# Memory updates, value copies, output gate and sample heads of a recurrent decoder's mixers, moved between engines and steps

## The chip, the core and the metric

The kernel runs on one core of a Trainium2 chip. Five engines work side by side, each through its own list of instructions in order: TensorE (PE, matrix products), VectorE (DVE), ScalarE (ACT), GpSimd (POOL) and SyncE (SP, which issues most transfers). They wait for each other on semaphores that the program sets by hand. The metric is the device time of one launch in microseconds (us); the median of three runs counts.

## What is computed

A two-layer decoder trunk for 256 prompt tokens and 8 sample sequences of 8 tokens, 320 columns in all, with the same weights. Each layer is a SwiGLU feed-forward part, a norm, one input projection, two mixers side by side (an RWKV-7 time mixer with 8 heads of 64 and an mLSTM with 4 heads of 128), an output projection, a norm, a second feed-forward part and a norm. All in fp32. The part of the reference that the change touches is the mLSTM's end of a chunk:

```python
num = g_inter[..., None] * einsum('bhtd,bhde->bhte', qc, C) + einsum('bhts,bhse->bhte', s, vc)
h = num / maximum(abs(den), exp(-m_t))[..., None]
C = dec[..., None, None] * C + einsum('bhs,bhsd,bhse->bhde', ws, kc, vc)
...
h = ((h - mu) * rsqrt(var + MH_EPS)).reshape(B, T, D_B) * mh_g
out = sigmoid(o_pre) * h
```

For the samples, `C` is a memory of 128 x 128 for each of 8 sequences and 4 heads, read from memory and written back with the layer's update. The RWKV-7 mixer is brought to a chunk form: per chunk of 64 tokens a triangular inverse is grown in six doubling levels, and a recurrence over four prompt chunks follows.

## The kernel before, in words

Each weight is split into a high and a low part (`whi` by ScalarE, `wlo` by VectorE) and multiplied in three passes (lines 2087 to 2089); the feed-forward parts and projections are such products. Between the input and the output projection of each layer lie the mixers, and there all that the change touches.

**The order of the mixers** is written out by hand. `tensor_mixers` (L916), `scalar_mixers` (L1226), `vector_mixers` (L1662) and `pool_mixers` (L1871) each run the same 27 steps, n = 0 to 26, one for each pair of level and chunk of the triangular inverse (five chunks, the fifth for the samples, with three levels). In a step n from 5 on TensorE makes a product (L735), VectorE masks it (L1684, `t1`), TensorE makes a growth from it in the next step (L747, L750), and ScalarE copies the growth (L1159); a growth waits for the copy of the one before. Steps 0 to 4 have a first growth only (L721, L724). All other work of the mixers hangs into these steps by tuples such as `WEIGHTS_AT`: the engine does it in that place of its list.

- **Side work** through bank 7 (`side` L666, `copy_side` L1127): TensorE turns or multiplies something, one of the other engines copies it out, and the next may start only then (`side_copied`). Number 0 is the tail of the projection, 1 to 5 the value tiles of the five chunks (copied into `uv`, two copies of 64 x 256, L1136), 6 to 10 the keys, 11 to 13 products of scores and values (`RVS`), 14 the last rows of the convolution (`ENDS`), 15 to 18 the states of the samples (`MEMS`).
- **The mLSTM** works in three tiles: two of 128 prompt tokens and one of the 64 sample tokens. Per tile TensorE makes scores (`tile_scores`, steps 9 and 14, the first ahead of step 0), VectorE the logarithms of weights (`tile_logs`), ScalarE exponentials (`tile_weights` L1086, in steps 4, 10, 15 at the end of the step), VectorE their product with the scores (`tile_products` L1447, steps 6, 11, 16), TensorE the numerators (`tile_values`, steps 7 and 12, `samples_of_heads`, steps 17 and 18). The tiles' heads are then normalised: means by VectorE (L1494), squares by ScalarE (L1109), spreads by VectorE (L1514), root by ScalarE (L1118), scaling by VectorE (L1528); group 0 is the prompt's 8 heads of 128 rows, group 1 the samples' 4 heads of 64 rows.
- **Left-overs** (`LEFT` L627, `left_over` L631, `left_over_done` L1538): thirteen small jobs through banks 4 to 6 in turn. "C" is the update of half a head's sample memories (a product of 64 x 128 by 64 x 512, then an addition by VectorE to `C0`), "H" turns a tile's heads back and VectorE multiplies them with the output gate `og`, "N" and "T" make and turn the normalisers. A job waits until the one three before has been taken from its bank.
- **The output gate** (`output_gate` L1078): a sigmoid over 128 x 1280 and four scalings with gains, by ScalarE ahead of step 0. Sigmoid, exponential and square root each need another table set, which the ScalarE loads.
- **POOL** makes the masks of values (L1848), multiplies the sample memories by their decays (L1855, eight operations, each awaited by the update of its half head through `memory_decayed`) and four memory terms of the RWKV-7 states (L1863, two operations each). It waits for semaphores in between, and it also issues output transfers.

The **recurrence** (`recurrence` L840, `scalar_recurrence`, `vector_recurrence`) follows the steps: for each of four chunks a product with the state, one with the inverse, one for the new state (L879), with copies by VectorE and ScalarE between. The left-overs 11 and 12 lie in its first chunk. SP sends a head's memories out when its second half is done (L2067), and waits for all of them before it loads the output projection's weights into the same place.

## Time and profile before

| | us |
|---|---|
| median of 3 runs (1552.19 to 1558.36) | 1557.95 |
| the profiled execution's own time | 1557.53 |
| its span, first to last instruction | 1555.8 |
| TensorE busy, of the span | 1487.7 (96%) |
| VectorE busy | 982.4 (63%) |
| ScalarE busy | 699.0 (45%) |
| POOL busy | 392.6 (25%) |
| mixers of layer 0, from the last product of the input projection to the end of the recurrence | some 379 to 507 |
| mixers of layer 1 | some 1144 to 1269 |

The difference between own time and span lies around the first and the last instruction. A busy TensorE is not TensorE at its peak: matrix products are pipelined, and the clock that they are granted is one of two levels, 2.4 GHz (1.00 in the profile) or 1.2 GHz (0.50). The rows that the prediction reads stand in a section of their own below.

### The profile page before, as it was taken

The numbers are of one execution on the slowest core, as the hardware profiler recorded it, in microseconds if no ns is written. First come the engines' busy times: TensorE is split into PE (matmuls) and PEld (weight loads), VectorE is DVE, ScalarE is ACT, GpSimd is POOL, SyncE is SP. The second block draws the span as 40 slices with busy tenths as digits, with TensorE's granted clock in tenths as the row PEclk, the third lists the DMA queues.
The fourth block names the chain that finished last, engine by engine and source line by source line (L and its number), as shares of the span: only waits on it lengthen the run. The fifth ranks groups of instructions, "written<-read, shape, count | busy, mean of one in ns | idle before, by whom it ended". The sixth has DMA issues, their size and how long they took to land.

```text
span 1555.8 us, 34010 instructions
## 1 busy us (share of the span) xinstructions
PE 1487.7 (96%) x13394; PEld 1430.9 (92%) x13394; DVE 982.4 (63%) x1519; ACT 699.0 (45%) x1200; POOL 392.6 (25%) x423
## 2 busy tenths in 40 slices
PE   8999999999888999999999999989998799999995
PEld 7999998999767999999999999979988589999995
DVE  4444445587265877775577775466854667877644
ACT  4333335755544543334443334366574355333332
POOL 4222472011441422220512221300143404222100
PEclk9999999999986999999999999999999799999998
DMA  8554543453113745454545545534421334545451
GB/s 216 148 149 148 164 148 81 133 139 83 31 32 91 193 136 148 143 153 150 155 126 148 155 139 165 153 96 119 120 58 30 108 92 143 174 137 159 150 163 34
DMA packets 318938, 198.82 MB, mean 128 GB/s; under 512 B 7792, under 2 KB 303760, under 8 KB 318832
## 3 DMA queue, kind: packets, MB, share of 16 engines
q1 hardware_dynamic: 315120, 190.69, 42.2%
q0 software_dynamic: 3712, 6.62, 2.1%
q8 instruction: 78, 1.28, 0.4%
q14 instruction: 28, 0.23, 0.0%
HBM read 188.50 MB, written 8.78 MB: 127 GB/s over the span
## 4 chain that ended last, share of the span: by engine, by line
PE 85%; DVE 7%; ACT 4%; DVEq 2%; issue 1%; DMA 0%; SPq 0%; ACTq 0%
PE bank L2087 23%; PE bank L2089 23%; PE bank L2088 23%; DVE wlo L2578 2%; PE bank L2174 1%; DVE rlo L2609 1%; ACT whi L2377 1%; PE bank L735 1%; PE bank L458 1%; PE bank L2179 1%; ACT z L1159 1%; PE bank L643 1%; PE bank L2138 1%; PE bank L747 1%; PE bank L750 1%
## 5 line engine op out<-in xcount | busy, mean ns | idle before, releaser
L2377 ACT ACTIVATE whi<-raw 128x1024 fp32r<-128x1024 f32 x340 | 358.2, 1059 | 470.5 <-PE bank L2089 451.4
L2578 DVE TENSOR_TENSOR wlo<-raw,whi 128x1024 fp32r<-128x1024 f32 x340 | 421.6, 1244 | 228.5 <-ACT whi L2377 227.7
L2087 PE MATMUL bank<-rhi,whi 128*128 128x322 f32 x984 | 306.5, 311 | 0.0
L2089 PE MATMUL bank<-rhi,wlo 128*128 128x322 f32 x984 | 305.9, 311 | 0.0
L2088 PE MATMUL bank<-rlo,whi 128*128 128x322 f32 x984 | 304.8, 310 | 0.0
L2087 PE MATMUL bank<-xh,whi 128*128 128x320 f32 x912 | 285.5, 313 | 4.1 <-DVE xl L2752 3.0
L2088 PE MATMUL bank<-xl,whi 128*128 128x320 f32 x912 | 282.4, 310 | 0.0
L2089 PE MATMUL bank<-xh,wlo 128*128 128x320 f32 x912 | 282.4, 310 | 0.0
L2847 POOL TENSOR_TENSOR hl<-scratch,hh 128x320 f32 x88 | 146.6, 1666 | 495.3 <-DVE scratch L2699 379.8
L2087 PE MATMUL bank<-hh,whi 128*128 128x320 f32 (+1 forms) x704 | 218.4, 310 | 0.5 <-DVE wlo L2578 0.5
L2089 PE MATMUL bank<-hh,wlo 128*128 128x320 f32 (+1 forms) x704 | 217.4, 309 | 0.0
L2088 PE MATMUL bank<-hl,whi 128*128 128x320 f32 (+1 forms) x704 | 217.4, 309 | 0.0
L2088 PEld LDWEIGHTS bank<-rlo,whi 128*128 128x128 f32 x984 | 186.5, 189 | 0.0
L2087 PEld LDWEIGHTS bank<-rhi,whi 128*128 128x128 f32 x984 | 185.5, 189 | 0.0
L2089 PEld LDWEIGHTS bank<-rhi,wlo 128*128 128x128 f32 x984 | 185.5, 189 | 0.0
L2087 PEld LDWEIGHTS bank<-xh,whi 128*128 128x128 f32 x912 | 172.3, 189 | 9.3 <-issue 6.3
L2088 PEld LDWEIGHTS bank<-xl,whi 128*128 128x128 f32 x912 | 172.4, 189 | 0.5
L2089 PEld LDWEIGHTS bank<-xh,wlo 128*128 128x128 f32 x912 | 172.3, 189 | 0.0
L2087 PEld LDWEIGHTS bank<-hh,whi 128*128 128x128 f32 x704 | 132.4, 188 | 1.3 <-issue 1.0
L2088 PEld LDWEIGHTS bank<-hl,whi 128*128 128x128 f32 x704 | 132.4, 188 | 0.2
L2089 PEld LDWEIGHTS bank<-hh,wlo 128*128 128x128 f32 x704 | 132.4, 188 | 0.0
L2680 DVE TENSOR_TENSOR scratch<-bank,scratch 128x322 f32<-128x322 f32 x132 | 65.0, 493 | 71.5 <-PE bank L2089 63.8
(420 smaller groups left out, 1963.9 us busy)
## 6 DMA issues: line engine op xcount, KB each, us to landing
raw<-in_ffn_wg SPq DMA_DIRECT2D x88, 512.0 KB, 3.8
raw<-in_ffn_wu SPq DMA_DIRECT2D x88, 512.0 KB, 3.8
raw<-in_ffn_wd SPq DMA_DIRECT2D x88, 512.0 KB, 3.6
raw<-in_w_in SPq DMA_DIRECT2D x60, 512.0 KB, 3.8
raw<-in_w_out SPq DMA_DIRECT2D x16, 512.0 KB, 5.5
raw<-in_state_C SPq DMA_DIRECT2D x8, 512.0 KB, 6.1
out_s_C<-raw SPq DMA_DIRECT2D x8, 512.0 KB, 3.9
ring<-in_state_wkv POOLq DMA_DIRECT2D x8, 256.0 KB, 5.1
```

The source lines that it names most:

```text
L458: return pe.matmul(out, src, ident[0:rows, 0:rows], start=True, stop=True)
L643: last = pe.matmul(b[:, :], kt[PART[q], 2, 2 * g, :], vmask[g][PART[q], 4 * half:4 * half + 4, :], start=True, stop=True)
L735: last = pe.matmul(bank[n % 2][PART[1 - q], j * CH:(j + 1) * CH], ati[part, c, j, :], xi(q, c, j), start=True, stop=True)
L747: pe.matmul(bank[2 + q][PART[q], j * CH:(j + 1) * CH], xti(q, c, j), t1[PART[1 - q], c, j, :], start=True, stop=True)
L750: last = pe.matmul(bank[2 + q][PART[1 - q], j * CH:(j + 1) * CH], t1[PART[1 - q], c, j, :], xti(q, c, j), start=True, stop=True)
L2087: pe.matmul(out, w_hi, hi, start=start, stop=False)
L2088: pe.matmul(out, w_hi, lo, start=False, stop=False)
L2089: return pe.matmul(out, w_lo, hi, start=False, stop=stop)
L2377: act.activation(whi[:, slot, :], raw[:, slot, :], ACT.Copy).then_inc(hi_ready.sem, 1)
L2578: dve.tensor_tensor(wlo[:, slot, :], raw[:, slot, :], whi[:, slot, :].bitcast(F32), ALU.subtract).then_inc(lo_ready.sem, 1)
L2680: dve.tensor_tensor(scaled, bank_of(L, f, d)[:, 0:T + 2], root, ALU.mult)
L2847: pool.tensor_tensor(at(hl), hval[:, k % 2, :], at(hh).bitcast(F32), ALU.subtract).then_inc(hl_done.sem, 1)
```

## The change

It has six parts. (1) The update of a half head is four operations on VectorE, one for each sequence: memory times its decay (a column of `rexp`) plus the product; POOL's decays and their semaphore are gone, and POOL masks the second pair of values as soon as the numerators are there. (2) The value tiles of side work are copied by VectorE (`copy_tokens`): the first four behind its last first-level mask and the first tile's logarithms, which move there too, the fifth behind step 5's mask. (3) The gate's sigmoid runs in ScalarE's step 16, the gains in step 17, and the exponential's table set is loaded ahead of step 0. (4) The exponentials of a tile run ahead of a step's growth copy from step 5 on, and those of the second and third tile in steps 9 and 14. (5) The sample heads' means, squares, spreads, root and scaling move from steps 24, 24, 25, 25, 26 to 20, 20, 21, 22, 23. (6) The turn of the sample heads becomes left-over 10, in step 25; the normalisers are made in step 26 and only their turn stays in the recurrence (L868 and, for VectorE, L1608). POOL's output transfers of memories and normalisers wait for the last left-over.

```diff
         LEFT = (("C", 0), ("C", 1), ("C", 2), ("C", 3), ("H", 0), ("H", 1), ("C", 4), ("C", 5), ("C", 6), ("C", 7),
-                ("N", 0), ("T", 0), ("H", 2))
+                ("H", 2), ("N", 0), ("T", 0))
...
@@ recurrence
                 if c == 0:
-                    left_over(pe, L, NLEFT - 2)
                     left_over(pe, L, NLEFT - 1)
...
-        LEFT_AT = (20, 20, 21, 21, 22, 22, 23, 23, 24, 24, 25, NSTEP, NSTEP)
+        LEFT_AT = (20, 20, 21, 21, 22, 22, 23, 23, 24, 24, 25, 26, NSTEP)
...
         def output_gate(act, L):
             act.activation(og[:, :, :], og[:, :, :], ACT.Sigmoid)
+
+        def output_gains(act, L):
             act.drain()
             for h in range(HB):
                 last = act.activation(og[:, h, :], og[:, h, :], ACT.Identity, scale=vec[:, V_MH + h:V_MH + h + 1])
...
@@ copy_side
-            elif k < KEYS:
-                for q in range(2):
-                    rows = PART[1 - q]
-                    last = act.activation(uv[rows, k - VALUES, :, q, :], heads4(b)[rows], ACT.Copy)
...
@@ scalar_mixers
-            output_gate(act, L)
+            act.preload_act_table_set("natural_log_exp_and_others")
             for n in range(NSTEP):
                 if n < NCH:
                     copy_growth(act, L, n)
-                if n in SIDE_AT:
+                if n in SIDE_AT and not VALUES <= SIDE_AT.index(n) < KEYS:
                     copy_side(act, L, SIDE_AT.index(n))
+                if n in WEIGHTS_AT:
+                    tile_weights(act, L, WEIGHTS_AT.index(n))
                 if n >= NCH:
                     copy_growth(act, L, n)
-                if n in WEIGHTS_AT:
-                    tile_weights(act, L, WEIGHTS_AT.index(n))
+                if n == GATE_AT:
+                    output_gate(act, L)
+                if n == GAINS_AT:
+                    output_gains(act, L)
...
-        WEIGHTS_AT = (4, 10, 15)
+        WEIGHTS_AT = (4, 9, 14)
-        SQUARES_AT = (17, 24)
-        ROOTS_AT = (19, 25)
+        GATE_AT, GAINS_AT = 16, 17
+        SQUARES_AT = (17, 20)
+        ROOTS_AT = (19, 22)
...
@@ left_over_done
             if kind == "C":
                 h, half = 2 * (i // 4) + i % 2, i // 2 % 2
-                own = C0[:, h, 4 * half:4 * half + 4, :].rearrange("p b e -> p (b e)")
-                dve.wait_ge(memory_decayed.sem, memory_decayed.by(L, i + 1))
-                last = dve.tensor_tensor(own, own, b[:, :], ALU.add)
+                for k in range(4):
+                    s = 4 * half + k
+                    at = h * TS + s * ST + ST - 1
+                    last = dve.scalar_tensor_tensor(out=C0[:, h, s, :], in0=C0[:, h, s, :], scalar=rexp[:, at:at + 1],
+                                                    in1=b[:, k * DK:(k + 1) * DK], op0=ALU.mult, op1=ALU.add)
...
+        def copy_tokens(dve, L, c):
+            dve.wait_ge(side_mm.sem, side_mm.by(L, VALUES + c + 1))
+            for q in range(2):
+                rows = PART[1 - q]
+                last = dve.tensor_copy(uv[rows, c, :, q, :], heads4(bank[7])[rows])
+            last.then_inc(side_copied.sem, 1)
...
@@ vector_mixers
+            tile_logs(dve, L, 0)
+            for c in range(NCH - 1):
+                copy_tokens(dve, L, c)
             for n in range(NCH, NSTEP):
                 lv, c = LEVELS[n]
                 if n in LOGS_AT:
-                    tile_logs(dve, L, LOGS_AT.index(n))
+                    tile_logs(dve, L, 1 + LOGS_AT.index(n))
                 dve.wait_ge(t1_mm.sem, t1_mm.by(L, n - NCH + 1))
                 tt(t1[:, c, :, :], heads4(bank[n % 2]), level_mask(lv), ALU.mult).then_inc(t1_ready.sem, 1)
+                if n == NCH:
+                    copy_tokens(dve, L, NCH - 1)
...
-        LOGS_AT = (5, 10, 15)
+        LOGS_AT = (10, 15)
-        MEANS_AT = (17, 24)
-        SPREADS_AT = (18, 25)
-        SCALED_AT = (20, 26)
+        MEANS_AT = (17, 20)
+        SPREADS_AT = (18, 21)
+        SCALED_AT = (20, 23)
...
@@ pool_mixers
             pool.wait_ge(num_mm.sem, num_mm.by(L, NTT))
-            decayed_memory(pool, L, 0)
-            decayed_memory(pool, L, 1)
             masked_values(pool, L, 1)
-            for i in range(2, 2 * HB):
-                decayed_memory(pool, L, i)
             pool.drain()
             pool.wait_ge(side_copied.sem, side_copied.by(L, MEMS))
             memory_term(pool, L, 1)
...
-            pool.wait_ge(left_done.sem, left_done.by(L, NLEFT - 1))
+            pool.wait_ge(left_done.sem, left_done.by(L, NLEFT))
```

## Rows read from the trace of the kernel before

**Rows 1.** The page, part 4: shares of the chain of waits by engine.
```profile
PE 85%; DVE 7%; ACT 4%; DVEq 2%; issue 1%; DMA 0%; SPq 0%; ACTq 0%
```

**Rows 2.** Timeline, ScalarE, layer 0: start us, us, engine, line, operation, out<-in, count [idle<-releaser].
```profile
388.91 1.28 ACT L1080 ACT_TABLE_LOAD   x1
390.20 1.27 ACT L1080 ACTIVATE scratch<-scratch 128x1280 f32<-128x1280 f32 x1
391.54 1.92 ACT L1083 ACTIVATE scratch<-scratch,vec 128x320 f32<-128x320 f32 x4
...
394.94 0.77 ACT L1136 ACTIVATE scratch<-bank 64x256 f32<-64x256 f32 x2 [0.23 <-PE bank L679]
...
400.37 1.28 ACT L1093 ACT_TABLE_LOAD   x1
...
402.99 0.64 ACT L1159 ACTIVATE z<-bank 128x256 f32<-128x256 f32 x2
```

**Rows 3.** Timeline, VectorE, layer 0: logs of the first tile; a copy of 64x256 from PSUM.
```profile
392.30 1.12 DVE L1436 SCALAR_TENSOR_TENSOR ring<-bank,scratch,negmask 128x128 f32<-128x128 f32 x4
...
474.88 0.42 DVE L1606 COPY scratch<-bank 64x256 f32<-64x256 f32 x1 [1.10 <-PE bank L864]
```

**Rows 4.** Timeline, VectorE, then TensorE, step 11 and 12: what they wait for.
```profile
420.57 0.69 DVE L1452 TENSOR_TENSOR scratch<-scratch,ring 128x512 f32<-128x512 f32 x1 [1.77 <-ACT ring L1093]
...
421.91 0.49 PE L593 MATMUL bank<-ring 128*128 128x129 f32 x2 [1.46 <-DVE ring L1454]
```

**Rows 5.** Timeline, VectorE, step 16: the queries of the third tile.
```profile
436.58 1.32 DVE L1452 TENSOR_TENSOR scratch<-scratch,ring 128x256 f32<-128x256 f32 x1 [1.66 <-ACT ring L1093]
```

**Rows 6.** Timeline, VectorE and POOL, step 18; the same kind later, in step 25.
```profile
444.79 1.90 DVE L1522 SCALAR_TENSOR_TENSOR scratch<-scratch 128x8 f32<-128x8 f32 x1
...
447.77 0.93 DVE L1526 TENSOR_SCALAR scratch<-scratch 128x8 f32<-128x8 f32 x1
...
470.27 0.15 DVE L1522 SCALAR_TENSOR_TENSOR scratch<-scratch 64x4 f32<-64x4 f32 x1
...
446.62 6.08 POOL L1861 TENSOR_TENSOR raw<-raw,ring 128x512 f32<-128x512 f32 x6
```

**Rows 7.** Timeline, VectorE, steps 13 to 24: memories, updates, products and small operations.
```profile
427.27 1.13 DVE L1469 SCALAR_TENSOR_TENSOR scratch<-scratch,ring,bank 128x129 f32<-128x129 f32 x4 [1.33 <-ACT ring L1107]
...
453.99 1.98 DVE L1536 TENSOR_TENSOR ring<-ring,scratch 128x1024 f32<-128x1024 f32 x1
455.90 1.27 DVE L1547 TENSOR_TENSOR raw<-raw,bank 128x512 f32<-128x512 f32 x2
...
465.28 1.03 DVE L1508 TENSOR_SCALAR scratch<-scratch 64x4 f32<-64x4 f32 x1
```

**Rows 8.** Windows, layer 0: us; PE, PEld, DVE, ACT, POOL busy (instructions); clock, DMA, GB/s.
```profile
451.60:473.70 22.10, 18.22 (x300) 12.67 (x300) 17.57 (x36) 9.27 (x22) 7.22 (x8) 0.81 0.34 97
...
467.60:469.30 1.70, 0.03 (x2) 0.00 (x0) 1.54 (x4) 0.63 (x1) 0.00 (x0) 0.97 0.00 0
469.30:493.00 23.70, 21.36 (x378) 19.69 (x378) 10.61 (x31) 8.22 (x22) 6.16 (x8) 0.50 0.51 147
493.10:508.00 14.90, 14.84 (x352) 11.04 (x352) 11.41 (x27) 10.77 (x29) 0.00 (x0) 1.00 0.01 3
```

**Rows 9.** Timeline, TensorE, recurrence of layer 0: sample heads' turn, state products (L879).
```profile
475.34 1.97 PE L458 MATMUL bank<-ident,ring 64*128 64x64 f32 x8
477.24 1.12 PE L879 MATMUL bank<-scratch 128*64 128x64 f32 x16
...
496.37 0.69 PE L879 MATMUL bank<-scratch 128*64 128x64 f32 x16
```

**Rows 10.** Timeline, TensorE, recurrence of layer 1: state products.
```profile
1240.02 1.12 PE L879 MATMUL bank<-scratch 128*64 128x64 f32 x16
...
1253.12 0.69 PE L879 MATMUL bank<-scratch 128*64 128x64 f32 x16
...
1257.78 0.69 PE L879 MATMUL bank<-scratch 128*64 128x64 f32 x16
```

More of the change, by code:

```diff
@@ L364, in hymba_kernel @@
         h_ready = signal("h_ready", 2)
-        memory_decayed = signal("memory_decayed", 2 * HB)
         vmask_ready = signal("vmask_ready", HB // 2)
@@ L1607, in vector_recurrence @@
                 if c == 0:
-                    left_over_done(dve, L, NLEFT - 2)
                     left_over_done(dve, L, NLEFT - 1)
@@ L1853, in masked_values @@
                                ALU.mult).then_inc(vmask_ready.sem, 1)
-        def decayed_memory(pool, L, i):
-            h, half = 2 * (i // 4) + i % 2, i // 2 % 2
-            own = C0[:, h, 4 * half:4 * half + 4, :]
-            at = h * TS + 4 * half * ST
-            decay_ = rexp[:, at:at + 4 * ST].rearrange("p (b t) -> p b t", t=ST)[:, :, ST - 1:ST]
-            pool.tensor_tensor(own, own, bcast(decay_, 2, DK), ALU.mult).then_inc(memory_decayed.sem, 1)
         def memory_term(pool, L, j):
```

## The prediction

> **What bounds the kernel now.** I read the chain of waits first: it lies on TensorE for 85% of the span [rows 1], nearly all of it the weight products of the feed-forward parts, which the change leaves alone. What it touches is one stretch in each of the two layers, the mixers: from about 389 to 478 us in layer 0, and the same again from 1154 us in layer 1. I then read that stretch engine by engine as a timeline, since there the chain hops between ScalarE, VectorE and TensorE and busy shares say little. Last I read the granted clock by stretches.
>
> The timeline shows five places. **(1)** ScalarE spends 388.91 to 393.46 on the output gate and keeps the first growth copy waiting, then copies five turned value tiles from 394.94 on, one per round of 1.55 us, then loads a table in the middle of this (400.37), so that the growth copy of step 5 comes at 402.99 [rows 2]. **(2)** In step 11 VectorE has idled 1.77 us for the exponential and TensorE 1.46 us for VectorE [rows 4]. **(3)** In step 16 the same wait is 1.66 us [rows 5]. **(4)** In step 18 three VectorE operations on 8 columns take 1.90, 0.93 and 0.93 us while POOL is on memory decays; the same kind takes 0.15 when POOL rests [rows 6]. **(5)** From step 20 on VectorE has 17.57 us of work in 22.1, the sample heads come last, TensorE stands almost empty (0.03 of 1.70 us) and is granted half the clock from 469.3 to 493.0, over most of the recurrence [rows 7, 8].
>
> **The change part by part, for one layer, in layer 0's times.** The profiled execution took 1557.53 us for a span of 1555.8, and it lies 0.4 below the median of the runs, 1557.95.
>
> (a) *Gate away from the front, value copies to VectorE.* The exponential's table now loads at 388.9 and is there at 390.2, before the first growth is; no load is left at 400.37. VectorE is on the logs until 393.42 [rows 3], so its first copy pair starts there. A copy of this shape takes 0.42 alone [rows 3], some 0.76 for two that overlap (ScalarE's two took 0.77 [rows 2]); the other 0.78 of a round, TensorE's turn and the ways between, stays. VectorE's copies then end at 394.2, 395.7, 397.2 and 398.8, the fifth turn at 399.4, the step-5 growth at 400.5, and ScalarE, free by then, copies it at 400.5 in place of 402.99: **−2.5**. Behind VectorE's waiting copies stands only its mask of step 5, whose product is not there before 398.5. Bounds: −1.3, if only the load of 1.28 goes, and −4.5, if the whole gate were on the chain.
>
> (b) *Second tile's weights in step 9 instead of 10.* The two exponentials run behind the logs and end before VectorE wants them. VectorE then goes as soon as step 11's mask is done. The wait that can go is TensorE's 1.46 [rows 4]; they now stand, with their wait for VectorE's logs, ahead of step 9's growth copy, which costs that a tenth or two where TensorE has its next turn to do: **−1.3**, bounds 0 and −1.5.
>
> (c) *Third tile's in step 14.* 1.66 can go, but there POOL masks values, and the product of 256 columns took 1.32 [rows 5] where 512 took 0.69 [rows 4]; it will only be held earlier. **−0.5**, bounds 0 and −1.7.
>
> (d) *Gate behind step 16, decays off POOL.* ScalarE has a gap there, but the gate asks 1.28 + 1.27 in step 16 and the gains 1.92 in step 17 [rows 2], and ahead of the head squares: these start some 0.8 later. Against this the three small operations took 3.76 together. POOL still has masked values and the first memory term (two operations of the decays' size, 1 us each: six took 6.08 [rows 6]); the latter is released by the copy of the last conv rows, right behind the squares, and so meets them again: two of three are held 1 us each, 2.2 in place of 3.8, with one more small gap saved: 1.2 to 1.6. **−0.4** net. Bounds: −3.3 (no lock, gate hidden) and +1.9 (gate in full, lock as before).
> The table load behind the gate is 1.28 in the row, and the sigmoid follows at once [rows 2].
> The Trainium skill (ScalarE: Activation LUTs, section What ACT_TABLE_LOAD costs) gives about 2.66 us for a switch, a drain included; by that the squares would come 1.4 later still and the sum below would be 2.8 smaller. No such drain stands in the row, so I keep 1.28.
>
> (e) *Memory updates and sample heads.* A half head was one operation, 0.64 (two took 1.27), and becomes four. The nearest row is the same form with 129 columns, in place: four took 1.13 [rows 7]. Eight times 0.49 is 3.9 more on VectorE a layer. The sample heads leave POOL's reach: an operation on 4 columns that took 1.03 takes 0.15 without POOL [rows 6, 7], another is like it, and the large product of the first heads, 1.98, and that of the sample heads may lose 0.8 and 0.7: in all −3.2 by estimate. So 17.57 becomes 18.3, and with half a microsecond of gaps VectorE alone sets this stretch: 18.8, and some 2.1 more for the last growth, its copy and the first product: 20.9 in place of 22.1. **−1.2**. Bounds: +3.9 (the operations added, nothing freed) and −3.3. POOL's memory terms three and two now fall in this stretch; the new operations read one tensor from PSUM, and the row of that form ran while POOL was idle, so I count no lock on them and keep it for the rivals. TensorE has left-overs to fill the time; SP sends the memories at the same points of the order as before, within a microsecond, and waits for them before the output weights, as now.
>
> (f) *Heads ahead of the normaliser.* In the recurrence's first step TensorE turned the sample heads for 1.97 us ahead of the state product at 477.24 [rows 9]. They go to step 25, where VectorE is the slower one; only the normaliser's turn stays, beside VectorE's copy (0.42 [rows 3]), which the state product may wait for some 0.2 longer. **−1.75**, bounds −1.5 and −2. POOL's wait moves from the twelfth left-over to the last, with three output DMAs and two more behind it; nobody wants these before the next feed-forward part.
>
> Engines in sum: −7.65 a layer, **−15.3** for two. Then the **clock**. The recurrence ran at 0.50 (1.2 GHz) from 469.3, right behind the emptiest stretch, and at 1.00 from 493.1 [rows 8]. From the first state product to the fourth were 19.1 us in layer 0 and 17.8 in layer 1, whose last step, at full clock, took 4.66; three such are 14.0 [rows 9, 10]. So 5.1 + 3.8 = 8.9 us would come back if (e) keeps TensorE fed and the clock up, and nothing if not; a new fall over one step would cost 1.7. The nearest row for a recurrence at full clock is the one from 493.1, which kept it; but one microsecond of error in (e) is enough to bring an empty stretch back. I take half, **−4.5**.
>
> 1557.5 − 15.3 − 4.5 = 1537.7, and 0.4 more against the median: **1538**. A half per cent (7.8 us, 1550.2) is about what a measurement of this kernel can tell from no change.
>
> **Rivals.**
> *Clock up in both recurrences:* 1557.5 − 15.3 − 8.9 + 0.4 = **1533.7**, down to 1528 if (d) also goes its whole way. For it: behind 493.1 TensorE was 14.84 of 14.90 us busy at 1.00 with the same kind of work [rows 8]. Against it: VectorE-bound steps leave holes. Chance 0.20.
> The Trainium skill (TensorE: Matmul & The Clock Gate, Part 1) has the low level as the default and activity as what releases it; by that alone this rival would be the likeliest. The falls behind empty stretches agree with it.
>
> *VectorE and POOL eat (c), (d) and (e), and the clock falls as before:* only (a), (b) and (f) are left, 5.55 a layer: 1557.5 − 11.1 + 0.4 = **1546.8**, 1542 to 1551. For it: each of three terms stands on a guess about who holds whom. Chance 0.25.
>
> *The table load does not leave the path* (a load still stands ahead of an exponential in steps 4 to 9, so that the preload does not do what it says) *and VectorE's copies make up the rest of (a):* with the rival before, 3.05 a layer: **1551.8**. Against it: the kernel preloads the same set elsewhere. Chance 0.06.
>
> *Slower: four small operations cost as much each as one large one.* Place: steps 20 to 24. At p us each, a layer pays 32p − 5.1. It is even with −7.65 at p = 0.40, and half a per cent slower at p = 0.52. At 0.64, the old price of 512 columns, it is +15.4 − 7.65 = 7.7 a layer: **1573**. Against it: 0.28 in the nearest row. Chance 0.05.
>
> **The numbers.** My forecast holds 0.44, from 1532 to 1542. The range runs from 1528 to 1549: it leaves out the load's and the slower rival, the top of the 1546.8 one and a tail below, about 0.19. Faster by over 0.5%: 0.44 + 0.20 + 0.22 = 0.86; within: 0.09; slower: 0.05.
>
> **What would show it.** Right: growth copy of step 5 some 11.6 us behind the first table load, not 14.1; no table load between step 0 and step 16; TensorE waiting under 0.3 us at the second value product; two, not three, long operations in step 18; updates near 0.28 each; no empty stretch ahead of the recurrence, the state products 4.7 apart with the clock at 1.00. Wrong: updates over 0.4; VectorE waiting for the squares behind the gains by over 2 us; a clock of 0.50 before the first state product.

## The result, and the profile after

The changed kernel took 1537.22 us (median of four runs, 1531.73 to 1540.04) against 1558.15 us before (1552.19 to 1558.50): a ratio of 0.987, 95% interval 0.9833 to 0.9907. The forecast was 1538.0 with a range from 1528 to 1549. The four runs of the changed kernel differ with the mean granted clock: 0.985 in the fastest, 0.973 in the slowest. The profiled execution is that fastest one, 1531.73 us for a span of 1530.0; before's was 1557.53. The gap between these two executions, 25.8 us, is thus some 5 us more than that of the medians, 20.9.

The page of the kernel after, its head and the shares of the chain:
```profile
span 1530.0 us, 34026 instructions
...
PE 1471.5 (96%) x13394; PEld 1414.8 (92%) x13394; DVE 988.6 (65%) x1587; ACT 692.8 (45%) x1180; POOL 379.2 (25%) x407
...
PE 83%; DVE 9%; ACT 4%; issue 2%; DVEq 1%; POOL 1%; DMA 0%; POOLq 0%; SPq 0%; ACTq 0%
```
VectorE's share of the chain is now 9% for 7% [rows 1]; the page's lines put 1% down to the updates, and what the rest is they do not say. "Issue" has doubled to 2%, which nothing in the forecast spoke of.

ScalarE in layer 0 after, as a timeline, with the columns of [rows 2]:
```profile
387.48 1.28 ACT L1229 ACT_TABLE_LOAD   x1
...
399.56 0.66 ACT L1156 ACTIVATE z<-bank 128x256 f32<-128x256 f32 x2 [2.48 <-PE bank L749]
...
430.07 1.28 ACT L1078 ACT_TABLE_LOAD   x1
...
435.44 1.04 ACT L1116 ACTIVATE spare<-ring 128x1024 f32<-128x1024 f32 x1
```
One load stands ahead of step 0 and none until the gate at 430.07. The growth copy of step 5 comes 12.08 us behind the first load in place of 14.08.

VectorE and POOL after, steps 18 and 24, from the same timeline:
```profile
437.80 0.67 DVE L1524 SCALAR_TENSOR_TENSOR scratch<-scratch 128x8 f32<-128x8 f32 x1
438.55 0.93 DVE L1526 TENSOR_TENSOR scratch<-scratch 128x8 f32<-128x8 f32 x1
439.55 0.17 DVE L1528 TENSOR_SCALAR scratch<-scratch 128x8 f32<-128x8 f32 x1
...
457.75 2.14 DVE L1550 SCALAR_TENSOR_TENSOR raw<-raw,ring,bank 128x128 f32<-128x128 f32 x8
...
437.41 2.04 POOL L1876 TENSOR_TENSOR scratch<-scratch,bmask 128x512 f32<-128x512 f32 x2 [0.91 <-ACT scratch L1143]
457.74 2.04 POOL L1876 TENSOR_TENSOR scratch<-scratch,bmask 128x512 f32<-128x512 f32 x2 [18.29 <-PE bank L642]
```
The three small operations of step 18 take 1.77 us together, 3.76 before [rows 6]; POOL's first memory term starts at 437.41 and holds two of them. Eight updates, at 457.75, take 2.14, 0.27 each, although a memory term runs beside them from 457.74. The Trainium skill (SBUF — State Buffer, section Who interferes with whom) has a VectorE instruction with two inputs from SBUF held by a POOL instruction that reads SBUF, and one with at most one not, outside the modes that use both of VectorE's ports. The rows agree with it: the two operations that are held have both inputs in SBUF, and the updates have their second tensor in PSUM. The third operation is no test, since it starts at 439.55, when POOL is done; it has one input, and before it took 0.93 us beside POOL all the same [rows 6], in which mode no row shows.

The recurrence of layer 0 after, on TensorE: the state products (L877), and what stands among them; first the product ahead of them (L863), with the idle time before it:
```profile
463.46 0.85 PE L863 MATMUL bank<-scratch,z 64*64 64x64 f32 x16 [0.86 <-ACT z L1156]
464.82 1.12 PE L877 MATMUL bank<-scratch 128*64 128x64 f32 x16
470.22 0.69 PE L877 MATMUL bank<-scratch 128*64 128x64 f32 x16
474.21 0.59 PE L789 MATMUL bank<-scratch 64*64 64x16 f32 x15 [1.81 <-issue]
476.28 0.69 PE L877 MATMUL bank<-scratch 128*64 128x64 f32 x16
480.94 0.69 PE L877 MATMUL bank<-scratch 128*64 128x64 f32 x16
```
And the windows of that stretch (columns as in [rows 8]):
```profile
442.60:463.50 20.90, 18.91 (x310) 13.10 (x310) 17.82 (x61) 9.12 (x23) 4.06 (x5) 0.90 0.36 102
462.70:466.90 4.20, 3.44 (x54) 2.82 (x55) 1.51 (x4) 1.12 (x4) 2.82 (x4) 0.63 0.47 136
466.90:472.40 5.50, 5.50 (x203) 5.32 (x204) 2.29 (x8) 2.38 (x8) 1.26 (x3) 0.97 1.03 308
472.40:474.20 1.80, 0.01 (x1) 0.00 (x0) 0.84 (x3) 1.35 (x2) 0.00 (x0) 1.00 0.62 184
474.20:489.30 15.10, 14.48 (x355) 11.09 (x356) 9.71 (x29) 11.01 (x33) 0.00 (x0) 1.00 0.02 6
```
The clock falls to 0.50 for 3.4 us at the start of the recurrence, 463.8 to 467.2, and is at 1.00 from there, where before it was 0.50 for 23.7 us [rows 8]. But at 472.4 TensorE stands 1.81 us with no wait that the trace can name; in layer 1 there is another such place of 1.24 us. The trace of before has none of them in the recurrence.

To compare all kernels I read six starts in every profiled execution, in both layers: ScalarE's last copy of the mLSTM's values (64x512; the zero: 388.30 before, 386.88 after, in layer 0), VectorE's mask of step 18, the last copy of numerators, the recurrence's first product, and its first and fourth state product. This is a table of differences of those starts, layer 0 / layer 1, in us:

| kernel | to the mask of step 18 | to the last numerators | to the recurrence | to the first state product | first to fourth |
|---|---|---|---|---|---|
| before | 54.16 / 51.27 | 8.37 / 8.36 | 22.89 / 23.55 | 3.52 / 3.52 | 19.13 / 17.76 |
| after | 47.95 / 47.96 | 7.01 / 7.00 | 21.62 / 21.61 | 1.36 / 1.45 | 16.12 / 15.97 |
| h2_back | 47.94 / 47.91 | 6.67 / 7.01 | 21.61 / 21.62 | 2.55 / 3.14 | 19.12 / 17.76 |
| heads_late | 47.95 / 47.95 | 7.01 / 7.02 | 23.36 / 23.33 | 3.51 / 3.52 | 19.02 / 18.41 |
| one_op | 47.95 / 47.76 | 7.84 / 7.85 | 21.22 / 21.22 | 1.64 / 1.20 | 15.67 / 13.82 |
| loads_later | 49.63 / 47.92 | 7.87 / 7.41 | 21.92 / 21.61 | 1.64 / 1.20 | 17.75 / 17.76 |
| gate_front | 51.67 / 50.00 | 6.30 / 6.74 | 22.08 / 21.62 | 1.64 / 1.20 | 19.49 / 16.49 |
| copies_act | 46.97 / 47.90 | 7.16 / 7.30 | 22.07 / 21.62 | 1.64 / 1.20 | 19.49 / 19.42 |
| keep_fed | 47.96 / 47.84 | 5.92 / 6.63 | 23.29 / 23.38 | 1.20 / 1.20 | 17.75 / 16.49 |
| keep_fed_loads | 47.96 / 47.91 | 5.92 / 5.92 | 24.98 / 24.96 | 1.20 / 1.20 | 13.70 / 13.70 |
| weights_fed | 50.65 / 50.62 | 6.78 / 6.78 | 23.28 / 24.99 | 1.20 / 1.20 | 13.70 / 13.69 |
| before_fed | 54.18 / 51.19 | 8.13 / 8.12 | 23.04 / 24.56 | 1.98 / 1.99 | 13.69 / 13.69 |
| end_fed | 47.42 / 48.26 | 5.91 / 5.31 | 22.36 / 22.37 | 1.20 / 1.20 | 13.70 / 13.69 |
| end_fed_one | 47.94 / 48.92 | 7.84 / 7.84 | 23.28 / 24.73 | 1.20 / 1.20 | 13.70 / 13.69 |

From before to after the rows differ by 14.0 us in layer 0 and 10.5 in layer 1; 1.4 more lie ahead of the first mixers, where the change does nothing. That makes the 25.8. Each row comes from one execution, so it holds clock as well as work: over both mixers TensorE stood at 0.50 for 71.7 us before and for 27.3 after.

### The profile page after: what moved, and what is told of

Same layout as the page of the kernel before. It is cut to its first block, busy times and chain, and to the rows that moved or that the text cites. A ratio compares the mean times of both kernels' runs of the same rounds, so it can differ in the third digit from the quotient of the medians.

```text
span 1530.0 us, 34026 instructions
## 1 busy us (share of the span) xinstructions
PE 1471.5 (96%) x13394; PEld 1414.8 (92%) x13394; DVE 988.6 (65%) x1587; ACT 692.8 (45%) x1180; POOL 379.2 (25%) x407
## 3 DMA queue, kind: packets, MB, share of 16 engines
q8 instruction: 78, 1.28, 0.3%
## 4 chain that ended last, share of the span: by engine, by line
PE 83%; DVE 9%; ACT 4%; issue 2%; DVEq 1%; POOL 1%; DMA 0%; POOLq 0%; SPq 0%; ACTq 0%
PE bank L2091 24%; PE bank L2093 23%; PE bank L2092 23%; DVE wlo L2582 2%; PE bank L2178 1%; DVE raw L1550 1%; DVE rlo L2613 1%; ACT whi L2381 1%; ACT z L1156 1%; PE bank L746 1%; PE bank L2183 1%; PE bank L835 1%; PE bank L831 1%; PE bank L570 1%; POOL spare L1899 1%
```

## The experiments

Theory: the change gains by its work, about 7.65 us a layer, and by keeping the clock up in the recurrence. Rivals: it gains by the clock alone; or the new updates cost as much as they free. Each kernel was timed in five rounds beside the kernel before; ratios are to that.

**heads_late and h2_back: where the sample heads stand.** In the first only their turn (H2) goes back into the recurrence, in the second the heads go back to their old steps as well.
```diff
-                ("H", 2), ("N", 0), ("T", 0))
+                ("N", 0), ("T", 0), ("H", 2))
 # heads_late, besides:
-        MEANS_AT, SPREADS_AT, SCALED_AT = (17, 20), (18, 21), (20, 23)
+        MEANS_AT, SPREADS_AT, SCALED_AT = (17, 24), (18, 25), (20, 26)
-        SQUARES_AT, ROOTS_AT = (17, 20), (19, 22)
+        SQUARES_AT, ROOTS_AT = (17, 24), (19, 25)
```


> The changed kernel with one thing undone: the sample heads' turn (H2) goes back into the first step of the recurrence, behind the normaliser; the sample heads themselves stay early. Theory (term f): the turn stands again between the first product of the recurrence and the first state product, 1.4 us apart in the changed kernel; they come 2.4 to 3.4 us apart, 1.0 to 2.0 a layer, 2 to 4 in all: 1539 to 1541 us. Rival (cover): VectorE's copy and its wait fill that time anyway, the first state product moves by under 0.4 us: 1537 to 1538. Rival (clock): more work for TensorE at this place brings the full clock sooner and gives back what the turn costs: the recurrence's 0.50 stretch of about 4 us ends sooner, 1535 to 1538.

> The changed kernel with the sample heads back at steps 24 to 26 and their turn in the recurrence; updates, gate, copies and weights stay as changed. Theory (terms e, f and the clock hang on the heads' place): TensorE stands empty again ahead of the recurrence, the clock is 0.50 over most of it, and from the first state product to the fourth take 18 to 19 us in layer 0 in place of 16.06; with the heads' chain of small operations back at the end (1 to 2 us) and the turn (1 to 2 us) a layer pays 4.5 to 7: 1546 to 1551 us. Rival (the clock hangs on the shorter updates or on POOL's rest, not on the heads): state products stay 16 us apart, only 2 to 3.5 a layer are lost: 1541 to 1544. Rival (nothing but clock luck): 1537.

h2_back took 1540.47 us (0.9894, 0.9877 to 0.9911), heads_late 1545.48 us (0.9925, 0.9909 to 0.9940). TensorE's timeline and windows, first of h2_back, then of heads_late:
```profile
464.40 1.67 PE L457 MATMUL bank<-ident,ring 64*128 64x64 f32 x8
...
465.00:481.00 16.00, 15.84 (x315) 15.15 (x317) 5.29 (x15) 6.24 (x16) 2.56 (x5) 0.50 0.51 151
```
```profile
461.59 1.12 PE L749 MATMUL bank<-z,spare 64*64 64x64 f32 x16 [2.86 <-DVE spare L1700]
...
465.60:486.50 20.90, 20.69 (x398) 19.31 (x400) 7.76 (x22) 7.09 (x20) 4.12 (x6) 0.54 0.39 116
```
heads_late came out nearly as the theory said, with a time 0.5 under the 1546 to 1551 expected: up to the last numerators it equals the changed kernel to a few hundredths, then it pays 1.7 in the stretch, 2.1 for the turn and 2.4 to 2.9 for the clock, which is 0.54 over the whole recurrence behind a TensorE that waits 2.86 us. So the sample heads' place is worth 6.3 to 6.8 a layer against the profiled execution of the changed kernel, 8.3 us in all by the medians. In h2_back the turn alone costs 1.2 and 1.7, and the recurrence runs 16 us at 0.50 although TensorE is full there (15.84 of 16): the rival by which more work would bring the clock back sooner is out. Its time hit the expected number, but with a part of it in the clock that the theory had not counted.

**one_op: the updates as before, decays on POOL.**
```diff
-                for k in range(4):
-                    last = dve.scalar_tensor_tensor(...)
+                dve.wait_ge(memory_decayed.sem, memory_decayed.by(L, i + 1))
+                last = dve.tensor_tensor(own, own, b[:, :], ALU.add)
...
+            decayed_memory(pool, L, i)   # two ahead of the second masked values, six behind
```


> The changed kernel with the memory updates as before: decays on POOL (eight of about 1 us), one VectorE operation of 512 columns for a half head (0.64) in place of four of 0.27. Theory (terms d and e): three small operations of step 18 take over 3 us again in place of 1.77, and the sample heads, now in steps 20 to 23, fall under POOL's decays as well: 2 to 4 us a layer against 8 x 0.45 = 3.6 us of VectorE saved: between no change and 4 us later in all for both layers, 1536 to 1541, with the gain of the change in place and not in price. Rival (the four operations are the bound): without them the stretch from the last numerators' copy to the recurrence, 20.9 us in the changed kernel, falls below 19.5, and the time is 1531 to 1535. Rival (the decays are late for the updates, and VectorE waits for POOL): 1542 to 1548.

It took 1537.16 us (0.9866, 0.9848 to 0.9885), level with the changed kernel. The table has both halves: 0.8 more ahead of the last numerators, where the three small operations took 2.59 (over 3 expected), and 0.4 less in the stretch behind. The price of four operations and what they free are about even here; neither rival with a larger effect stands. Its profiled execution also has a recurrence at full clock without a gap, in layer 1 (13.82), to which the part on the gap comes back.

**gate_front and copies_act: the two halves of term (a).** The gate ahead of step 0 with the copies left to VectorE; the copies on ScalarE with the gate left behind step 16.
```diff
 # gate_front
-            act.preload_act_table_set("natural_log_exp_and_others")
+            output_gate(act, L)
+            output_gains(act, L)
 # copies_act
-                if n in SIDE_AT and not VALUES <= SIDE_AT.index(n) < KEYS:
+                if n in SIDE_AT:
```


> The changed kernel with the output gate and its gains back ahead of step 0 (a table load, the sigmoid, the gains), and so a load for the exponentials in steps 0 to 4 again; the value copies stay with VectorE. Theory (terms a and d): the growth copy of step 5 comes 1.3 to 2.5 us later behind the first table load (12.1 in the changed kernel, 13.4 to 14.6 here), and the squares of step 17 come 1 to 1.3 us sooner against the rest, since VectorE waits 1.25 us for them there now: between 0 and 1.5 us a layer lost, 1537 to 1540. Rival (the gate costs more behind step 16 than ahead of step 0): 1533 to 1536. Rival (the load alone is hidden, the front does not move): 1534 to 1536.

> The changed kernel with the five turned value tiles copied by ScalarE again; the gate stays behind step 16. Theory (term a: what stood in the way was the gate, not who copies; ScalarE's two copies took 0.77 where VectorE's take 0.86 and ScalarE has nothing else between the first growths): rounds of 1.55 us in place of 1.65, the growth copy of step 5 0 to 0.6 us sooner behind the table load, no difference that can be told in the time: 1535 to 1538. Rival (ScalarE's copies hold its growth copies and the first exponentials): growth copy of step 5 1 to 2 us later, 1539 to 1542.

gate_front took 1541.40 us (0.9893, 0.9876 to 0.9910), copies_act 1538.85 us (0.9888, 0.9870 to 0.9905), 1.4 and 0.9 over the ranges expected. ScalarE's timeline in gate_front:
```profile
389.10 1.28 ACT L1078 ACT_TABLE_LOAD   x1
...
400.24 1.28 ACT L1094 ACT_TABLE_LOAD   x1
401.53 0.63 ACT L1094 ACTIVATE ring<-ring 128x512 f32<-128x512 f32 x1
403.35 0.66 ACT L1156 ACTIVATE z<-bank 128x256 f32<-128x256 f32 x2 [1.19 <-PE bank L749]
```
The second load is back and the growth copy comes 14.25 behind the first, 2.2 later than in the changed kernel (1.5 in layer 1): the whole of term (a) that the trace shows is the gate. That VectorE copies the values is worth nothing by itself; with ScalarE the mask of step 18 comes 0.1 to 1.0 sooner, and the time cannot be told from the changed kernel's.

**loads_later, keep_fed, keep_fed_loads: the gap and the clock.** The loads of the output weights held until the third state product; products that nobody reads added where TensorE waits; both.
```diff
 # loads_later, on SP
+                sp.wait_ge(s_mm.sem, s_mm.by(L, 3))
                 each(sp, WO, KT, lambda p, i: load(p, i, columns(I["w_out"], ...)))
 # keep_fed, on TensorE: b is bank[5] in step 18, the left-over's own, bank[7] ahead of the recurrence
+            for _ in range(count):          # 14; 3 and 3; 5
+                pe.matmul(b[:, 0:P], ident[:, :], ident[:, :], start=True, stop=True)
```


> The changed kernel, with the queue of SP holding the four loads of the output weights until the third product of the states. In the changed kernel TensorE stands 1.81 us (layer 0) and 1.24 us (layer 1) in the recurrence, at full clock, with no wait that the trace shows, while these loads fill the DMA engines and a packet of the instruction queue is under way. Theory: TensorE waits for its instructions behind those loads; with the loads later both gaps are gone, the first to fourth state product take about 14.3 us in layer 0 in place of 16.06, and the time is 3 us lower, 1533 to 1535. Rival (the gap is a property of the engine or of that place in the code): it stays, 1537. Rival (the loads become the wait): they land about 486 to 487, just when ScalarE wants to split them, or meet another fetch of instructions: the gap moves and the time is 1537 to 1540.

> The changed kernel with products added that nobody reads, written to idle PSUM banks: 14 of 128x128x128 ahead of TensorE's 3 us wait in step 18, three ahead of each of the left-overs 10 and 11 (steps 25 and 26), five ahead of the recurrence. Theory (the clock falls behind the stretches where TensorE has little to do, and each fall into the recurrence costs): the 0.50 stretch behind step 18 and the one at the start of the recurrence are gone or under 3 us in both layers, state products first to fourth take 14.3 to 15.8 us, and the runs lie together, median 1529 to 1533. Rival (the granted clock does not follow what TensorE does here): falls as in the changed kernel, 1536 to 1541. Rival (the added work itself stands in the way, 14 x 0.17 = 2.3 us in step 18 where TensorE waits 3.1): growth of steps 18 and 26 later by over 0.5 us, 1536 to 1540 in spite of a full clock.

> The same with the four loads of the output weights held until the third product of the states. Theory of the gap (TensorE at full clock waits for its instructions behind these loads): the stretch of 1.2 to 1.8 us in the recurrence in which TensorE stands with no wait shown, there in the kernel with added products and in the changed one, is gone or below 0.4 us, and the time is 1.5 to 3.5 us under the kernel with added products alone: 1526 to 1531. Rival (not the loads): the gap stays, same time. Rival (the loads come too late at full clock): ScalarE waits for them ahead of the split of the output weights, time up by 1 to 3 us.

loads_later took 1538.56 us (0.9867, 0.9845 to 0.9889), keep_fed 1536.88 us (0.9878, 0.9860 to 0.9897), keep_fed_loads 1530.95 us (0.9832, 0.9818 to 0.9846), its five runs within 1.4 us. loads_later settles nothing: in its profiled execution the recurrence fell to 0.50 in both layers, so there was no full clock for a gap to show in. The pair with the added products does. Windows of keep_fed in the recurrence of layer 0, and the line on which TensorE resumes:
```profile
465.30:470.70 5.40, 5.35 (x186) 5.15 (x186) 2.64 (x8) 1.33 (x5) 2.57 (x5) 1.00 0.82 234
470.70:472.80 2.10, 0.05 (x3) 0.02 (x2) 0.58 (x2) 0.91 (x4) 0.00 (x0) 1.00 1.09 347
472.80:479.60 6.80, 6.65 (x142) 6.16 (x144) 2.88 (x9) 4.00 (x9) 0.00 (x0) 0.59 0.22 65
...
472.79 0.45 PE L787 MATMUL bank<-scratch 128*64 128x64 f32 x6 [2.05 <-issue]
```
The same of keep_fed_loads:
```profile
466.80:480.50 13.70, 12.67 (x416) 11.82 (x417) 8.21 (x24) 7.27 (x19) 2.53 (x5) 1.00 0.27 74
```
In keep_fed the clock is up at the start of both recurrences, as the theory said; then the gap comes (2.05 us, and 1.79 in layer 1), and behind the empty stretch the clock falls to 0.59. So the theory was right on the clock and wrong on the time.

One part of the reason is the new fall behind the gap. The larger is the third rival, which holds in part: the recurrence's first product comes 1.7 us a layer later behind the last numerators than in the changed kernel (23.29 and 23.38 for 21.62 and 21.61), in layer 0 with the clock at 1.00 from 432 to 472, and in that stretch the added products stand. The two layers make 3.4 of the 3.7 us by which the profiled execution, 1535.42, is slower than the changed kernel's.

With the loads out of the way there is no gap in either layer, the clock stays at 1.00, and first to fourth state product take 13.70 twice; the time is 5.9 under that of keep_fed, where 1.5 to 3.5 had been expected. A gap does not always bring a fall: behind both gaps of the changed kernel and that of one_op the clock stayed at 1.00 (474.2 to 489.3 in layer 0 of the changed kernel); behind both of keep_fed and the last of gate_front it fell.

What the trace shows of the gap itself is the traffic. DMA queues of the kernel after from 466.0 to 472.4, packets, MB, share of 16 engines:
```profile
q1 hardware_dynamic: 3315, 1.67, 91.3%
q0 software_dynamic: 134, 0.26, 10.7%
q8 instruction: 1, 0.02, 1.0%
```
One packet of the instruction queue is among loads that fill all engines. The same view from 471.7 to 472.8, around that packet alone:
```profile
q1 hardware_dynamic: 599, 0.30, 94.4%
q8 instruction: 1, 0.02, 5.6%
```
In the trace this packet ends at 472.75, and TensorE resumes 1.46 us later. In every gap of a recurrence, two shorter ones in layer 1 of gate_front included (0.57 and 0.89 us), it resumes 1.29 to 1.51 us behind the end of such a packet. No wait in the trace names the packet, so that TensorE waits for it is shown only as far as times can show it.

The loads by themselves do not bring a gap. Layer 1 of one_op has them at their old place and the clock at 1.00, and no gap; a window, and the queue from 1219.7 to 1221.4:
```profile
1220.00:1224.00 4.00, 4.00 (x154) 3.90 (x155) 1.89 (x6) 1.33 (x5) 1.77 (x3) 1.00 1.04 302
q8 instruction: 1, 0.02, 5.9%
```
There the packet started 1.49 us behind the first state product, just as the loads began to fill the engines (DMA share 0.12 from 1218 to 1220). In keep_fed it started 4.97 and 5.55 us behind that product, among the loads; in keep_fed_loads 2.07 and 3.19, without them. So the gap goes with a packet that comes behind the loads.

The Trainium skill (Runtime: NRT & Kernel Launch, section Instruction fetch mechanics) calls the cost of crossing a block of instructions "mostly hidden"; if these gaps are such crossings, it was not hidden in them, at 0.57 to 2.05 us. Nor are the output weights' loads the only way to such a gap: end_fed has one of 1.13 us in layer 1 at 1162.26, among POOL's loads of states, and resumes 1.26 us behind a packet; keep_fed and end_fed_one have shorter ones near that place.

**weights_fed and before_fed: the work, with the clock kept up.** The second and third tile's weights at their old places, on top of keep_fed_loads; and the kernel before with added products and later loads.
```diff
 # weights_fed
-        WEIGHTS_AT = (4, 9, 14)
+        WEIGHTS_AT = (4, 10, 15)
 # and tile_weights behind copy_growth of the step again
```


> The changed kernel with added products and later loads (1531), with the second and third tile's weights back behind the growth copies of steps 10 and 15. Theory (terms b and c): TensorE waits again for VectorE's products, some 1.5 us in step 11 and some 1.7 in step 16, and the squares come 1.3 to 3 us later behind the first copies of the keys: 2.6 to 6 us in both layers, 1533.5 to 1537. Rival (the two places gain nothing; the stretch from step 7 to 16 is shorter in the changed kernel because the half clock there is shorter): 1530.5 to 1532, and the squares within 0.5 us.

> The kernel before, with products added that nobody reads (20 ahead of TensorE's wait in step 18, 10 and 5 ahead of the last two growths, 4 ahead of the recurrence) and the loads of the output weights held until the third product of the states, that is the kernel before at full clock and with its instructions in time. Theory (the change gains by its work, 7.65 a layer as forecast, and the clock comes on top): the state products come 4.6 us apart from first to fourth (13.7 in place of 19.1 and 17.8), the turn of the sample heads takes 1.0 in place of 1.97, and the time falls by 10 to 14 us: 1544 to 1548, still 13 to 17 us over the changed kernel with the same two additions (1531). Rival (the gain of the change is mostly the clock): 1534 to 1539, within 8 us of it. Rival (the added products don't keep the clock here): 1553 to 1558.

weights_fed took 1537.49 us (0.9871, 0.9849 to 0.9894), 6.5 more than keep_fed_loads and 0.5 over the range expected. What waits in it, VectorE and TensorE by the timeline:
```profile
415.34 0.69 DVE L1464 TENSOR_TENSOR scratch<-scratch,ring 128x512 f32<-128x512 f32 x1 [1.78 <-ACT ring L1104]
416.69 0.49 PE L592 MATMUL bank<-ring 128*128 128x129 f32 x2 [1.46 <-DVE ring L1466]
433.15 0.60 PE L608 MATMUL bank<-scratch 128*64 128x8 f32 x8 [0.66 <-DVE ring L1466]
```
The waits of [rows 4] and a part of that of [rows 5] are back, and the mask of step 18 comes 2.7 later in both layers. These 2.7 hold a fall of the clock that keep_fed_loads does not have (0.51 and 0.50 for 3.4 us, from 425.8 in layer 0 and 1180.2 in layer 1), so the weights' steps alone are worth less. before_fed took 1546.00 us (0.9930, 0.9911 to 0.9949): its recurrence ran at full clock, 13.69 from first to fourth in both layers, and its time is 15.05 over that of keep_fed_loads, the changed kernel with the same kind of additions. Over both mixers the two stood at 0.50 for 17.1 and 20.5 us, so that the clock is nearly equal in them. The rival by which the change gains mostly through the clock is out.

**end_fed and end_fed_one: a faster version, and the updates' price in it.** Later loads, six added products (two at left-over 11, four ahead of the recurrence), and POOL's first memory term held; then the same with the old updates.
```diff
+            pool.wait_ge(hvar_ready.sem, hvar_ready.by(L, 1))
             memory_term(pool, L, 1)
```


> The changed kernel with later loads of the output weights, only six of the added products (two ahead of left-over 11, four ahead of the recurrence), none in step 18, and POOL holding its first memory term until the variances of step 18 are there. Theory (POOL's memory term holds the small operations of step 18; four products ahead of the recurrence are enough for the clock): these operations take 0.17 each in place of 0.67 and 0.93, the recurrence starts 0.8 to 1.5 us sooner behind the first copies of the keys than in the changed kernel (79.97), state products first to fourth in about 13.7 us without a gap: 1526 to 1530. Rival (six added products don't keep the clock up): the recurrence falls to 0.50 again, 1532 to 1537. Rival (the late memory term holds the sample heads' operations instead): the recurrence starts no sooner, 1530 to 1532.

> The fastest kernel so far (1525: later loads, six added products, POOL's first memory term behind the variances), with the memory updates as before the change: decays on POOL, one VectorE operation for a half head. With the recurrence at full clock in every run the price of this part can be read from the time. Theory (terms d and e: the four operations cost 8 x 0.45 = 3.6 us more of VectorE, and freeing step 18 and the sample heads from POOL gives back that and a little more): the small operations of step 18 take 0.7 to 0.9 each again, those of the sample heads up to 1.1, updates 0.64 to 0.68; the recurrence starts 0.3 to 1.8 us later a layer: 1526 to 1529. Rival (the four operations cost more than they free): it starts sooner, 1520 to 1524. Rival (nothing either way, less than 0.3 us a layer): 1524.5 to 1526.

end_fed took **1525.13 us** (1524.69 to 1526.98; 0.9796, 0.9777 to 0.9814), the fastest of all kernels here. Its step 18 on VectorE, and a window over its recurrence:
```profile
439.73 0.17 DVE L1532 SCALAR_TENSOR_TENSOR scratch<-scratch 128x8 f32<-128x8 f32 x1
439.97 0.17 DVE L1534 TENSOR_TENSOR scratch<-scratch 128x8 f32<-128x8 f32 x1
440.22 0.17 DVE L1536 TENSOR_SCALAR scratch<-scratch 128x8 f32<-128x8 f32 x1
...
464.40:480.00 15.60, 14.40 (x458) 13.18 (x458) 8.93 (x26) 8.20 (x23) 4.00 (x6) 1.00 0.28 76
```
All three small operations are free, and with six added products the clock was at 1.00 in both recurrences. The 5.8 us against keep_fed_loads are not the memory term's: there the three operations take 0.17 each too, since the 14 added products of step 18 push that term behind them (439.59). end_fed has fewer added products in the stretch ahead of the recurrence (22.36 for 24.98 in layer 0) and stood at 0.50 for 13.7 us of both mixers, keep_fed_loads for 20.5. end_fed_one took 1535.03 us (0.9853, 0.9837 to 0.9869), 9.9 more by the medians and 8.9 by the ratios, where 1 to 4 had been expected. VectorE in it:
```profile
438.48 0.73 DVE L1533 SCALAR_TENSOR_TENSOR scratch<-scratch 128x8 f32<-128x8 f32 x1
439.29 0.93 DVE L1535 TENSOR_TENSOR scratch<-scratch 128x8 f32<-128x8 f32 x1
440.29 0.93 DVE L1537 TENSOR_SCALAR scratch<-scratch 128x8 f32<-128x8 f32 x1
...
457.19 0.17 DVE L1543 RECIPROCAL scratch<-scratch 64x4 f32<-64x4 f32 x1 [0.71 <-ACT scratch L1133]
...
460.56 1.29 DVE L1558 TENSOR_TENSOR raw<-raw,bank 128x512 f32<-128x512 f32 x2 [0.68 <-PE bank L645]
```
Two things add up there. POOL's decays take back what the held memory term had freed: 2.59 for the three operations in place of 0.51, and 1.9 and 2.5 more to the last numerators by the table. And with a wait of 3.94 us in step 18 (2.45 and 1.85 in end_fed) the clock falls for longer, 34.1 us at 0.50 in both mixers for 13.7, in layer 1 most of 1192 to 1209 us, so that VectorE now waits for TensorE between the updates (0.68) and the stretch is 0.9 and 2.4 longer with less VectorE work in it. The same part was worth nothing in the changed kernel (one_op), where the memory term holds two of the three operations in any case. How much of the 9.9 is the clock was not separated further.

## Why the prediction was right, point by point

The figures by term below are read from one execution of each kernel, and as said above they hold clock as well as work. The cleanest pair is before_fed and keep_fed_loads.

**(a) Gate and copies, −2.5 forecast.** Measured −2.0 in both layers (growth copy of step 5: 12.08 for 14.08). The step that was a little off is the copies' round: VectorE's two took 0.86 and not 0.76, so a round is 1.65 us and not 1.55. copies_act bears this out: with ScalarE's round the growth copy comes 11.64 us behind the load, the 11.6 of the forecast. gate_front gives 2.2 and 1.5 back. That VectorE takes the copies, which this term had as a part of the gain, was not borne out: copies_act shows that it does not matter.

**(b), (c) Weights in steps 9 and 14, −1.3 and −0.5.** weights_fed puts them at 2.7 a layer against 1.8. The trace has 1.5 of it up to the second numerators' copy (16.87 for 15.34 behind the first), with one fall of the clock in each kernel: that is (b), nearly as forecast. The other 1.2, from there to the mask of step 18, holds the further fall of weights_fed, so that (c) is not shown apart. The fear of POOL, which held (c) down to 0.5, was right in part: POOL's lock on the third tile's product fell from 1.32 to 0.89, but the four operations on 128x64 behind it took 0.86 and 2.05 us a pair, 0.34 before. TensorE's wait at the second value product, 1.46 before, is under 0.15, as the sign said. Between before and after these stages differ by 4.2 in layer 0 and 1.3 in layer 1, with the clock falling at other places.

**(d) Gate behind step 16, decays off POOL, −0.4.** Measured −1.36, inside its bounds. The small operations fell by 2.0, as worked out (two of three held), and the squares came 0.65 later rather than 0.8 with the gains in front; VectorE waited 1.25 for them. In end_fed the stage is 1.1 and 1.7 shorter again, but keep_fed_loads has 1.1 of this in both layers without the hold on the memory term; what the clock has in it, which falls from 439.9 in the changed kernel, was not separated.

**(e) Updates and sample heads, −1.2.** Measured −1.27 and −1.94, with more half clock before than after; VectorE was 17.82 us busy in the 20.9 that the forecast gave for the stretch, and an update took 0.27 (0.28 forecast). With added products in both and the clock nearly equal no gain is left (before_fed 23.04 and 24.56, keep_fed_loads 24.98 and 24.96), so that the size of this term is not shown. The slower rival (p of 0.52) was nowhere near. Its sum counts the updates' 3.9 us twice, since −7.65 holds them already: at 0.64 a layer would pay 3.85 and not 7.7, and the rival would stand at 1565.6.

**(f) Sample heads ahead of the normaliser, −1.75.** Measured −2.2 and −2.1. h2_back says what it hangs on: 1.2 to 1.7 when put back, the more the lower the clock; between before_fed and keep_fed_loads it is 0.8.

**The clock, −4.5.** From first to fourth state product −3.0 and −1.8 in the profiled execution, 4.8 in sum. The size is right for this, the fastest execution; loads_later and copies_act, profiled at a mean clock of 0.973, have 17.75 to 19.49 there, which gives nothing back. The way to it was not as forecast: half was taken because one microsecond of error could bring a fall back. What came is a fall of 3.4 us at the start of the recurrence, and a gap of 1.8 and 1.2 us that was in no term. Of the signs named, "no empty stretch ahead of the recurrence" held only in part (0.86 us are left), the state products were 5.4, 6.1 and 4.7 apart, and the clock was at 0.50 before the first state product, which had been put down as a sign against the forecast. It did not cost as much as that sign supposed, because the fall lasted 3.4 us and not 24.

**The sum.** Work of 15.3 was forecast; before_fed against keep_fed_loads gives 15.05, but the agreement is partly chance. By stages, layer 0 and 1, that pair gains 6.2 and 3.3 to the mask of step 18, 2.2 and 2.2 in (d), 0.8 and 0.8 in (f), and loses 1.9 and 0.4 in the stretch, which in keep_fed_loads is 3.4 us a layer longer than in the changed kernel (24.98 for 21.62). The profiled execution of the changed kernel shows 19.7 by engine terms and 4.8 by the clock, more than forecast; the median lies 5.5 us behind it, with a lower clock in the other runs. So the nearness of the median to 1538 is partly luck too: terms that came out larger, against a clock that was lower. The rival with the clock up in both recurrences (1533.7) fits the fastest run, 1531.73, by its number alone, for its recurrences took 16.12 and 15.97 and not 14. The Trainium skill's figure for the table load (ScalarE: Activation LUTs, section What ACT_TABLE_LOAD costs; 2.66) would have made the gain smaller. The load behind step 16 stands at 1.28 in the row, as taken, and the sigmoid follows it at once, at 431.37.

## What to carry to other kernels

A stall that ends in an idle TensorE can be paid twice, once as the wait and once in the clock behind it, and the second part comes and goes between runs: make the candidates equal in clock (added products that stand in no one's way), and check how long each stood at half clock, before their work is compared. A part that frees an engine is worth only what the next holder of that engine leaves: the decays' removal gave nothing in the changed kernel, and 9.9 us, clock included, once the memory term was moved. When a stage becomes faster, look at which transfers now fall into it; here loads that had been harmless at half clock opened a gap at full clock, where they came ahead of a packet of instructions.

## What the runs showed of the hardware that was not expected

TensorE stood 0.57 to 2.05 us with no wait in the trace in six recurrences (both of the kernel after and of keep_fed, layer 0 of one_op, layer 1 of gate_front), each at full clock and with the output weights' loads still ahead of it, and resumed 1.29 to 1.51 us behind the end of an instruction packet. It did not in the ten recurrences of keep_fed_loads, weights_fed, before_fed, end_fed and end_fed_one with these loads moved (13.69 to 13.70 each), nor in layer 1 of one_op, where the packet came just as the loads began.

Falls of the clock do not all need an empty stretch. Two windows of the kernel after:
```profile
407.20:409.20 2.00, 2.00 (x18) 1.88 (x17) 0.00 (x0) 0.00 (x0) 0.00 (x0) 1.00 1.08 191
409.20:412.60 3.40, 3.40 (x56) 2.84 (x54) 1.48 (x5) 1.89 (x4) 0.00 (x0) 0.50 0.51 89
```
From 409.2 to 412.6 us it was at 0.50, while TensorE had been busy through the 2 us before; end_fed has no fall at that place and one at 425.7. In h2_back the clock stayed at 0.50 for 16 us of full TensorE work, in the kernel after for 3.4; what sets that length is open.
